# RMS norms: two tiles of the next layer computed from the unnormalised residual, the factor applied to their results

## The reference

```python
def rms_norm(x, g):
    y = x * lax.rsqrt(jnp.mean(x * x, axis=-1, keepdims=True) + EPS)
    return y * g

for layer in range(2):
    sh1, sc1, g1, sh2, sc2, g2 = adaln_params(c, ada_w[layer], ada_b[layer])
    h = rms_norm(x, norm_mix_g[layer]) * (1.0 + sc1) + sh1
    # layer 0: a recurrence and a stick-breaking attention; layer 1: windowed attention,
    # whose q, k, v come from h @ od_w_in, q and k normalised per head of 64
    x = x + g1 * mix
    h = rms_norm(x, norm_ffn_g[layer]) * (1.0 + sc2) + sh2
    x = x + g2 * conv_ffn(h)      # (silu(conv3(h @ w_gate)) * (h @ w_up)) @ w_down
```

## Time and profile before

| what | value |
|---|---|
| median of 3 runs | 3556.76 us (3547.88 to 3561.09) |
| the profiled execution, its own time | 3565.12 us |
| its span in the profile | 3563.2 us |
| mean granted TensorE clock | 0.98 |
| busy: PE, VectorE, ScalarE, GpSimd | 97%, 47%, 39%, 42% |

### The profile page before, as it was taken

One profiled execution on the slowest core, in us unless ns is written; L12 is line 12 of the kernel. 1 busy time (PEld: TensorE's weight loads), 2 busy tenths in 40 slices (PEclk: granted clock), 3 DMA queues, 4 the chain that ended last, 5 costly groups with the idle time before them and its releaser, 6 DMA issues.

```text
span 3563.2 us, 39161 instructions
## 1 busy us (share of the span) xinstructions
PE 3453.3 (97%) x15922; PEld 2734.3 (77%) x15922; DVE 1678.2 (47%) x2224; ACT 1374.1 (39%) x2273; POOL 1487.5 (42%) x803
## 2 busy tenths in 40 slices
PE   7999999999999999999999999999899999999999
PEld 5887667877888788776787878876578787778887
DVE  3437564355542443756436454556557512443320
ACT  3544444223322444444423422255532223643321
POOL 3233434444554433344544454442244544125543
PEclk9999999999999999999999999999999999999999
DMA  6333212543554333321244455431135533113332
GB/s 218 104 116 119 66 42 60 153 133 118 175 166 119 105 101 113 124 60 46 80 141 130 142 160 156 118 91 58 36 101 171 147 97 93 51 54 101 95 93 73
DMA packets 566994, 385.33 MB, mean 108 GB/s; under 512 B 13606, under 2 KB 504310, under 8 KB 566814
## 3 DMA queue, kind: packets, MB, share of 16 engines
q1 hardware_dynamic: 564574, 379.58, 36.0%
q10 hardware_dynamic: 2240, 3.25, 0.3%
HBM read 379.27 MB, written 2.10 MB: 107 GB/s over the span
## 4 chain that ended last, share of the span: by engine, by line
PE 79%; DVE 10%; ACT 4%; DMA 3%; POOL 2%; issue 1%; SPq 0%; ACTq 0%; DVEq 0%; POOLq 0%
PE ps L179 78%; DVE ACC L154 2%; POOL wlo L146 1%; DMA raw<-in_w 1%; PE ps L183 1%; ACT whi L142 1%; DVE mq L154 1%; ACT L138 1%; DVE H L154 1%; DVE np L146 1%; DMA raw<-in_ffn_w_gate 0%; DMA raw<-in_ffn_w_up 0%; SPq L176 0%; DVE sp L154 0%; DVE ACC L150 0%
## 5 line engine op out<-in xcount | busy, mean ns | idle before, releaser
L146 POOL TENSOR_TENSOR wlo<-raw,whi 128x1024 fp32r<-128x1024 f32 (+1 forms) x540 | 1276.1, 2372 | 1774.0 <-ACT whi L142 1745.7
L179 PE MATMUL ps<-UH,whi 128*128 128x512 f32 x2656 | 1058.8, 399 | 5.3 <-ACT VA L142 2.7
L179 PE MATMUL ps<-UH,wlo 128*128 128x512 f32 x2656 | 1040.2, 392 | 10.3 <-POOL wlo L146 10.3
L179 PE MATMUL ps<-UL,whi 128*128 128x512 f32 x2656 | 1039.7, 391 | 0.7 <-DVE UL L146 0.6
L142 ACT ACTIVATE whi<-raw 128x1024 fp32r<-128x1024 f32 (+1 forms) x540 | 549.4, 1026 | 786.6 <-PE ps L179 348.0
L179 PEld LDWEIGHTS ps<-UH,whi 128*128 128x128 f32 x2656 | 501.5, 189 | 125.3 <-issue 13.5
L179 PEld LDWEIGHTS ps<-UH,wlo 128*128 128x128 f32 x2656 | 501.6, 189 | 124.0 <-POOL wlo L146 15.5
L179 PEld LDWEIGHTS ps<-UL,whi 128*128 128x128 f32 x2656 | 501.2, 189 | 108.9 <-DVE UL L146 2.6
L154 DVE SCALAR_TENSOR_TENSOR ACC<-raw,SM,ACC 128x512 f32<-128x512 f32 x308 | 363.9, 1181 | 20.5 <-DVE ST L160 0.5
L179 PE MATMUL ps<-GH,whi 128*128 128x512 f32 x704 | 275.6, 391 | 0.0
L179 PE MATMUL ps<-GH,wlo 128*128 128x512 f32 x704 | 274.4, 390 | 0.3 <-POOL wlo L146 0.3
(11 more groups left out here) (368 smaller groups left out, 4232.0 us busy)
## 6 DMA issues: line engine op xcount, KB each, us to landing
raw<-in_w_in SPq DMA_DIRECT2D x168, 512.0 KB, 3.7
raw<-in_w SPq DMA_DIRECT2D x120, 512.0 KB, 5.2
raw<-in_ada_w SPq DMA_DIRECT2D x96, 512.0 KB, 4.7
raw<-in_w_ada SPq DMA_DIRECT2D x80, 512.0 KB, 4.7
raw<-in_ffn_w_gate SPq DMA_DIRECT2D x44, 512.0 KB, 3.8
raw<-in_ffn_w_up SPq DMA_DIRECT2D x44, 512.0 KB, 3.8
raw<-in_ffn_w_down SPq DMA_DIRECT2D x32, 512.0 KB, 3.9
raw<-in_ev_w_in SPq DMA_DIRECT2D x20, 512.0 KB, 3.7
```

What stands on the lines that cost most here:

```text
L146: return self.e.tensor_tensor(o, a, b, op).then_inc(*self.done(*keys))
L179: m = self.e.matmul(o, l, r, start=start, stop=stop)
```

## The change

- At `n6`, `n7`, `n8` two jobs (`f1` 0 and `f2` 0, or the two key tiles) are made from x*S. During the residual ScalarE writes `UH` = rounded H*S (`act_early_hi`, one more activation for each tile) and VectorE the remainder (`dve_early_lo`). `pe_early_norm` runs tiles 0 to 2 of the first job, the columns of the last square, tiles 3 to 7, the spreading matmul, then the whole second job. The dummy matmuls are gone.
- ScalarE copies the factor from the bank to `N1`. `dve_early_norm` makes H*r for the normal `UH` and `UL`, which go over the early ones once the second job has read them (key `vk`), and multiplies the two results by r (`dve_early_out`), adding the shift term to all but `f2` 0, where it goes into the product.
- Three further jobs then run beside the norm: `f1` 1, `f2` 1, `f1` 2, or the query tiles 0, 1, 2, with the key sums of squares put before tile 6 of them. So the spreading of the key factor follows directly.
- The shift term sh @ w of the six early tiles is made during earlier fills: at six calls n = 4 (units at 29, 30, 36, 37, 40, 41) the weight chunk is loaded once more, unsplit, VectorE does eight dependent 128x128 multiply-adds on it, PE sums with a one-column matmul and VectorE copies the column.

The diff, cut to its core:

```diff
+    SHIFTS = {29: ("n6", 0), 30: ("n6", 1), 36: ("n7", 0), 37: ("n7", 1), 40: ("n8", 0), 41: ("n8", 1)}
@@ pe_fill
+        if n == 1 and at - 1 in SHIFTS:
+            pe_shift(p, *SHIFTS[at - 1])
-        if n < 4:
+        if n == 4 and at in SHIFTS:
+            ada_chunk[SHIFTS[at]] = take((False,) + shift_weights(*SHIFTS[at]))
+        elif n < 4:
@@ dve_fill
+        if n == 4 and at in SHIFTS:
+            dve_shift_sums(v, *SHIFTS[at])
+    def dve_shift_sums(v, nid, j):
...
+        for k in range(NT):
+            w, x = raws[i % NRAW][:, k * 128:(k + 1) * 128], ad(blk, jsh, k, 1)
+            if k:
+                v.wait_ge(*v.prior())
+                v.stt(CP[:, j, :], w, x, CP[:, j, :], ALU.mult, ALU.add, *([("acd", i), ("cw", nid, j)] if k == NT - 1 else []))
+            else:
+                v.ts(CP[:, j, :], w, x, None, ALU.mult, None)
...
+    def dve_early_out(v, nid, j):
+        v.wait_ge(*on("pe", EARLY[nid][j]))
+        v.wait_ge(*on("act", "rs", nid))
+        v.tt(t, ps(EARLY[nid][j])[:, :], N1[:, :], ALU.mult, ("z", nid, j))
+        if nid == "n7" or j == 0:
+            v.ts(t, t, shift_column(nid, j), None, ALU.add, None, ("zc", nid, j))
...
+    def pe_early_norm(p, nid, jobs):
+        js = [pe_open(p, *job) for job in jobs]
...
+        pe_part(p, js[0], range(3), UH, UL, scaled)
+        p.wait_ge(*on("act", "sq", nid, NT - 1))
+        pe_column(p, nid, 4, N3, False, ("c2", nid))
+        pe_part(p, js[0], range(3, NT), UH, UL, scaled)
+        o = bank(p, AUX, ("R", nid), ("act", ("rs", nid)))
+        p.wait_ge(*on("dve", "dg", nid))
+        p.mm(o[:, :], ones, N2[:, :], True, True, ("R", nid))
+        pe_part(p, js[1], range(NT), UH, UL, scaled, lambda k: [("vk", nid, k)])
+    def dve_early_norm(v, nid):
+        v.wait_ge(*on("pe", "c2", nid))
+        v.ts(SQC, ps(("st", nid))[:, 4:8], 1.0 / D, None, ALU.mult, None, ("var", nid))
+        dve_early_lo(v, nid, NT - 1)
+        v.wait_ge(*on("act", "sd", nid))
+        v.recip(RC, RC)
...
+        dve_diagonal(v, nid, N2, RC)
+        for kt in range(NT):
+            v.wait_ge(*on("pe", "vk", nid, kt))
+            v.wait_ge(*on("act", "rs", nid))
+            v.tt(UF[:, kt, :], H[:, kt, :], N1[:, :], ALU.mult, ("h", nid, kt))
+            if kt in (1, 4):
+                dve_early_out(v, nid, kt // 4)
+            if kt:
+                put_lo(v, nid, kt - 1)
...
+    def act_early_norm(a, nid, first):
+        act_root(a, nid, EPS_RMS)
+        act_split(a, lin_end[first] + 4)
+        a.wait_ge(*on("pe", "R", nid))
+        a.cp(N1[:, :], ps(("R", nid))[:, :], ("rs", nid))
+        for kt in range(NT):
+            act_u(a, nid, kt, False)
+            if kt == 0:
+                act_split(a, lin_end[first] + 5)
+            if kt in (3, 5) and nid == "n7":
+                act_key_squares(a, kt // 4)
...
@@ pe_ffn
+        if early:
+            pe_early_norm(p, nid, [x[:4] + (("dve", ("z", nid, j)), LIN4) for j, x in enumerate((one(0), two(0)))])
+        first = (one(1), two(1), one(2)) if early else (one(0), two(0), one(1))
+        pe_beside_norm(p, nid, [x + (LIN4,) for x in first])
@@ pe_odd
-        pe_beside_norm(p, nid, [(("ok", i), "od_w_in_2", 0, 1024 + 128 * i, ("act", ("ok", i)), LIN4) for i in range(2)] +
-                       [(("oq", 0), "od_w_in_2", 0, 0, ("act", ("oqs", 0)), LIN4)])
-        pe_head_sums(p, ("k",), lambda i: T["ksq"][i], 2, T["RG"], O_AUX)
-        q(1, LIN4)
-        q(2, LIN4)
+        pe_early_norm(p, nid, [(("ok", i), "od_w_in_2", 0, 1024 + 128 * i, ("dve", ("z", nid, i)), LIN4) for i in range(2)])
+        pe_beside_norm(p, nid, [(("oq", i), "od_w_in_2", 0, 128 * i, ("act", ("oqs", i)), LIN4) for i in range(3)],
+                       {6: lambda: pe_head_sums(p, ("k",), lambda i: T["ksq"][i], 2, T["RG"], O_AUX)})
         pe_head_spread(p, ("k",), 2, T["RG"], O_AUX)
```

More of the change, by code:

```diff
@@ L372, in pe_open, with pe_part @@
         return key, o, i
-    def pe_part(p, job, ks, XH, XL, xw):
+    def pe_part(p, job, ks, XH, XL, xw, each=lambda k: ()):
         key, o, i = job
@@ L384, in pe_part @@
             p.wait_ge(*xw(k)[1])
-            p.mm(o[:, :], wh, XL[:, k, :], False, k == NT - 1, *([("used", i), key] if k == NT - 1 else []))
+            p.mm(o[:, :], wh, XL[:, k, :], False, k == NT - 1, *each(k), *([("used", i), key] if k == NT - 1 else []))
     WHOLE = [(slice(128 * b, 128 * b + 128), [(b, 0, 128)]) for b in range(4)]
@@ L484, in dve_fill @@
             add_biases(v, g)
+        if n == 2 and at - 1 in SHIFTS:
+            dve_shift_out(v, *SHIFTS[at - 1])
+        if n == 4 and at in SHIFTS:
+            dve_shift_sums(v, *SHIFTS[at])
         if at >= len(FILL) or n == 4:
@@ L883, in pe_norm, with early_tile, act_early_hi @@
         pe_spread(p, nid, N2, 0 if means else 1)
+    EARLY = {"n6": (("f1", 2, 0), ("f2", 2, 0)), "n7": (("ok", 0), ("ok", 1)), "n8": (("f1", 3, 0), ("f2", 3, 0))}
+    Z = [at("Z0", 86, [128, S]), at("Z1", 84, [128, S])]
+    def early_tile(nid, j):
+        return OD["KT"][:, j, 128:640] if nid == "n7" else Z[j][:, :]
+    def act_early_hi(a, rid, nid, m):
+        a.wait_ge(*on("dve", "mod", nid))
+        a.wait_ge(*on("dve", "H", rid, m))
+        a.af(UH[:, m, :], H[:, m, :], ACT.Identity, ("vh", nid, m), scale=S1[:, m:m + 1])
@@ new lines, in act_early_norm, with pool_early_norm @@
+    def act_early_norm(a, nid, first):
[9 more added lines that the diff above has]
+                act_key_squares(a, kt // 4)
+    def pool_early_norm(g, nid, first):
+        pool_split(g, lin_end[first] + 5)
+        for kt in range(NT):
+            put_lo(g, nid, kt)
@@ L895, in pe_spread, with pe_beside_norm @@
         pe_busy(p, ps(("st", nid)), 3)
-    def pe_beside_norm(p, nid, jobs):
+    def pe_beside_norm(p, nid, jobs, inside={}):
         js = [pe_open(p, *job) for job in jobs]
         for k in range(NT):
+            if k in inside:
+                inside[k]()
             for job in js:
@@ L917, in act_sq @@
         a.wait_ge(*on("dve", *(("Hc", nid) if means else ("H", rid)), m))
-        if 1 < m < NT - 1:
+        if 1 < m < NT - 1 or nid in EARLY and m > 1:
             a.wait_ge(*on("dve", "add", nid, m - 1))
-        a.af(UF[:, m, :] if m == NT - 1 else (N3 if m else N2)[:, :], H[:, m, :], ACT.Square, ("sq", nid, m))
+        a.af(UF[:, m, :] if m == NT - 1 and nid not in EARLY else (N3 if m else N2)[:, :], H[:, m, :], ACT.Square,
+             ("sq", nid, m))
     def dve_bias(v, nid, b, keep, scaled_before):
@@ L1145, in pe_residual @@
             pe_turned(p, rid, NT - 1)
-        elif nid != "n4":
+        elif nid != "n4" and nid not in EARLY:
             pe_norm(p, nid, sums == "means")
@@ L1152, in dve_residual @@
         added = {3: (1,), 4: (2,), 5: (3, 4), 6: (5,)}
+        early = nid in EARLY
+        if early:
+            beside()
         for m in range(NT):
@@ L1157, in dve_residual @@
                 dve_add(v, nid, NT - 2)
-                beside()
+                if not early:
+                    beside()
+            if early and m:
+                dve_early_lo(v, nid, m - 1)
             v.wait_ge(*kept(m))
@@ L1196, in act_residual @@
                 act_sq(a, rid, nid, means, m)
+                if nid in EARLY:
+                    act_early_hi(a, rid, nid, m)
             elif sums == "turned" and m:
@@ L1202, in act_residual @@
         act_sq(a, rid, nid, means, NT - 1)
+        if nid in EARLY:
+            act_early_hi(a, rid, nid, NT - 1)
     def pool_residual(g, rid, third):
@@ L1968, in copy_vm, with taps @@
                      *([("VM", lay, half, b)] if x else []), accum_out=ml[lay]["VS"][:, b, h:h + 1])
-    def taps(v, q, key, n, mid, w, b, last):
-        o = ps(key)
+    def taps(v, q, key, n, mid, w, b, last, src=None):
+        o = src or ps(key)
         v.ts(q[:, 0:S], o[:, :], w(mid), b, ALU.mult, ALU.add)
@@ L2295, in two @@
             return ("f2", f, m), n2, T["lay"], 128 * m, ("dve", ("fm", f, m))
-        pe_beside_norm(p, nid, [x + (LIN4,) for x in (one(0), two(0), one(1))])
+        early = nid in EARLY
+        if early:
+            pe_early_norm(p, nid, [x[:4] + (("dve", ("z", nid, j)), LIN4) for j, x in enumerate((one(0), two(0)))])
+        first = (one(1), two(1), one(2)) if early else (one(0), two(0), one(1))
+        pe_beside_norm(p, nid, [x + (LIN4,) for x in first])
+        done = [x[0] for x in first]
         for m in range(1, FT):
@@ L2300, in pe_ffn @@
                 pe_fill(p)
+            if one(m)[0] not in done:
                 pe_lin(p, [one(m)], NT, UH, UL, None, LIN4)
             pe_fill(p)
-            pe_lin(p, [two(m)], NT, UH, UL, None, LIN4)
+            if two(m)[0] not in done:
+                pe_lin(p, [two(m)], NT, UH, UL, None, LIN4)
     def act_ffn(a, f, scaled):
@@ L2347, in dve_ffn @@
             v.wait_ge(*on("act", "fs", f, m))
+            if m == 0 and nid in EARLY:
+                v.wait_ge(*on("dve", "z", nid, 1))
```

(12 more changed lines are left out.)

50 lines of the change are left out of this document (39 added, 11 removed).

## The result

The changed kernel takes 3571.3 us (median of 6 runs, 3564.3 to 3578.3), the kernel before 3553.3 beside it (6 runs): ratio **1.0049** [1.0036, 1.0062]. That is slower, though just within the 0.5% that I had called no change, and above the range, which ended at 3568. So the two profiles lie only 3.8 us apart in span while the medians lie 18.0 apart, and stages have to be compared over several kernels, which the experiments give.

The account below looks back on a forecast made before the run. PE, busy for 97% of the span, was taken to bound the kernel. Terms of -5.8 (n8), -2.5 (n7), 0 (n6), +4.5 (shift loads) and +2 (added matmuls) gave -1.8 us: median 3555, range 3542 to 3568.

Parts of the forecast that it names:

- The gap: At each norm, PE's lost stretch of 7.65 us (n6, n7) or 9.04 (n8) shrinks to 2.7 of columns and spreading.
- the rival of the port keeping the factor back: At each norm, diagonal or first scaling meets the added split, costing 2.4 us; 3560 us in all, chance 12%.
- n8, forecast -5.8: At n8, before FFN 3, the 6.3 us gap gain is kept, less 0.5 for the port.
- they cost nothing while DVE and ACT idle there: In the residuals, the extra early tile (0.81 us) and remainder (0.75) lie beside a job of 5.44 us or more: free.
- n7, forecast -2.5: At n7 and attention, a gain of 3.0 us despite a new 4 us wait, less 0.5 for the port.
- From there to the first scores it is the same 15 us: In attention, the time from spreading the key factor to the first scores stays 15 us, ending in the KD wait.
- n6, forecast 0: At n6, FFN 2 is fed at its limit, so the 4.95 us gained are gone within three steps.
- the shift load at unit 37 delays the next one by 2.4: In FFN 2 behind n6, the shift load delays the next load by 2.4 us, so up job 3 starts unchanged.
- The shift loads, forecast +4.5: In FFN 1 and FFN 2, four of the six loads cost 0.5, 1.2, 1.3 and 1.5 us.
- The second rival: A starved ring at the fills of FFN 1 and FFN 2: 5 us a miss, four misses, 3570 us, chance 16%.
- The added columns, forecast +2: Six one-column matmuls among PE's jobs cost 0.33 us each, their waits being on sums made some steps earlier.
- The port, 0.5 us a norm: At each norm, DVE instructions with two SBUF inputs contend with POOL's splits, priced at 0.5 us.

Follow-up runs that it names:

- e2: The kernel before with the shift loads, sums, one-column matmuls and copies added at the change's six calls, their columns unused: ratio 1.0042 to the kernel before.
- e13: The kernel before with ScalarE issuing the eight KD copies ahead of the root of the first queries: ratio 0.9987 to the kernel before.
- e1: The changed kernel without shift loads, sums, one-column matmuls and copies, so the early tiles lack their shift term: ratio 0.9987 to the kernel before.
- e3: The changed kernel with ScalarE and POOL splitting three chunks of FFN 2 behind n6 one step earlier: ratio 1.0042 to the kernel before.
- e4: The changed kernel with the four shift loads of n7 and n8 moved behind the last fill, n6's two kept: ratio 1.0008 to the kernel before.
- e5: The kernel of e4 with the root of the key sums ahead of query tile 0 on ScalarE: ratio 1.0007 to the kernel before.
- e7: The kernel of e4 with the eight scalings reading the factor from its PSUM bank instead of N1: ratio 1.0008 to the kernel before.
- e6: The kernel of e4 with the early remainder moved behind the next tile's sum of squares on DVE: ratio 0.9995 to the kernel before.
- e9: The kernel of e8 with ScalarE's rounding of the mask moved behind the root of the key sums: ratio 0.9977 to the kernel before.
- e10: The kernel of e9 with the scalings reading the factor from its PSUM bank: ratio 0.9979 to the kernel before.
- e12: The kernel of e9 with ScalarE issuing the eight KD copies ahead of the root of the first queries: ratio 0.9974 to the kernel before.
- e11: Early tiles at n8 alone, with two shift loads instead of four, everything at n7 as before: ratio 0.9989 to the kernel before.
- e8: Early tiles at n7 and n8 only, shift loads moved as in e4, orders of e5 and e6: ratio 0.9986 to the kernel before.

## Why the prediction was wrong, point by point

- **The gap.** Right at n6 and n7: 1.0 us from the last residual matmul to the first useful one (below 1.5 forecast), 2.1 us of columns and spreading (2.7 forecast). At n8 it was 3.5 us, by the wait at the columns. PE waits for the diagonal at none of the three, so the rival of the port keeping the factor back is excluded.
- **n8, forecast -5.8; measured -1.2 in one profile, and nothing in groups** (before, e2 and e13, with the old n8, average 248.7; after, e1, e3, e4 and e5 average 249.3; e7, with the same wait of 2.2 us but less of the lower clock behind it, has 246.1). The step that failed: "they cost nothing while DVE and ACT idle there", of the early tile and its remainder. DVE was idle before them, but they closed a loop with the sum of squares, which takes 2.49 us beside POOL's split, not 0.69. I had listed this port for four kinds of instruction and not for this sum. With the loop opened (e6 and five more) the stage has 242.9 us, 5.8 below those 248.7: the gap was there to win, its cover was not. That this is the forecast to a tenth is partly luck, since the 248.7 hold a half clock that comes or not: in the first 15 us of the stage the granted clock is 0.77 in before, 0.89 in e13 and 1.00 in e2, whose 247.4 leave 4.5 us for the gap alone.
- **n7, forecast -2.5; measured +0.8.** The wait for `ORG` was forecast at 4 us and took 3.94. Two steps failed. "From there to the first scores it is the same 15 us": it took 19.4, at half clock for its first 9.5 us; this was an end of mine, and I gave it no weight in the sum. And the root had two predecessors, of which I named one. With both moved behind it the gain is 4.5 us (e9, e10 and e12 against before, e2 and e11), and ends on the copies of `KD`.
- **n6, forecast 0.** The early tiles themselves seem to have gained a little: the five kernels with them and without the shift loads of units 37 to 41 in FFN 2 (e1, e4 to e7) have 254.2 us on average (251.5 to 256.1), the seven with n6 as before and without those loads (before, e8 to e13) 256.9 (255.1 to 259.6), so 2.7 us, against 3.7 for their own two loads in FFN 1. In the changed kernel this was hidden by the next point. The step "the shift load at unit 37 delays the next one by 2.4" failed in size and in kind: sums of 5.8 us, and an order by chunk numbers on ScalarE that I had not looked at.
- **The shift loads, forecast +4.5; measured +14.4 by e2's median, +16.8 by stages.** This term made the result. FFN 1 3.7; r3 4.8 (129.5 in after, e2 and e3, 124.7 on average in the others); FFN 2 8.3 (e2 with n6 as before, 265.2, against 256.9). The steps: "its job of 66 matmuls covers it" at unit 36 (the load behind the sums is needed 4.3 us after it goes out, however long the job), 2.4 us for a chain of sums (3.0 to 7.6), and a slack of "1 to 3 us", which chains 0.6 to 5.2 us longer than that used up (argued from where PE stopped, not measured by itself). The second rival, at 16%, named the mechanism and nearly the total, 3570. Its parts came out differently: 3.7 us for the two loads of FFN 1, where it had 5 for each, 8.3 for the three of FFN 2, 4.8 in r3, where it had none, and n7 and n8 without the 9 us that it took off. That these sum to 3571 is partly luck. No run takes the load, its sums and its column apart, so which of the three costs how much stays open; that the place decides is shown by e4.
- **The added columns, forecast +2.** No term of its own can be told apart. But that their waits "are on sums made some steps earlier" was false once PE ran ahead: 7.21 us in e3.
- **The port, 0.5 us a norm**: at the scalings the pause of PE is about that (0.85 between starts less 0.23), and no gain in the total can be seen without it (e7, e10). The rule that I took from the Trainium skill (SBUF — State Buffer, "Who interferes with whom") holds in the rows here: `np<-np,np`, `UF<-H,np` and the `CP` sums, all of SBUF inputs, are longer beside POOL's split, `UF<-H,ps` keeps 0.64 to 0.69. The page makes an exception for instructions with one SBUF tensor in the two-port modes, which my summary of it left out: the first step of a chain, `CP<-raw,AD`, took 1.76 us beside a split in FFN 1 against 0.28 alone. I listed scalings, diagonal, early remainders and shift sums under the rule, but priced only the scalings, which mattered least, and did not list the sum of squares.
- **The sum.** By stages, one profile each, -0.2 + 4.1 + 6.9 + 0.8 - 1.2 = +10.4; FFN 1's mean instead of its one lucky profile makes this about +14, against 18.0 of the medians. The last 4 us lie within what stages of unchanged code vary by from run to run.
